# Overflow blocks moved behind the last expert's combine and written out, first rows turned ahead of two tables

## The reference, cut to what matters

```
g_sel = argmax(softmax(xf @ w_group + b_group))                 # 1 of 4 groups
top_w, top_i = top_k(softmax(e_logits of that group), 2)        # 2 of its 4 experts
for e in range(16):
    h = silu(xf @ w_gate[e]) * (xf @ w_up[e])                   # 2048 -> 512
    y = y + combine[:, e:e + 1] * (h @ w_down[e])               # 512 -> 2048
```

## Time and profile before

| | us |
|---|---|
| median of 3 runs (lowest, highest) | 1303.7 (1301.46, 1304.48) |
| the profiled execution, its own time | 1306.76 |
| its span, first to last instruction | 1304.8 |
| PE busy | 1225.2 (94%) |
| DVE busy | 490.5 (38%) |
| ACT busy | 190.3 (15%) |
| POOL busy | 51.1 (4%) |
| DMA, mean over the span | 254 GB/s |

### The profile page before, as it was taken

The page is one execution under the profiler, slowest core; times in us unless marked ns, Lnnn a source line. Parts: engine busy times, 40 slices in busy tenths (PEclk is TensorE's granted clock), DMA queues, the critical chain, the costliest instruction groups (busy, mean ns, idle before and its releaser), DMA issues.

```text
span 1304.8 us, 13620 instructions
## 1 busy us (share of the span) xinstructions
PE 1225.2 (94%) x5624; PEld 587.2 (45%) x5624; DVE 490.5 (38%) x958; ACT 190.3 (15%) x397; POOL 51.1 (4%) x67
## 2 busy tenths in 40 slices
PE   6999999999999977999997979999999999999995
PEld 4344443344444454777785764333333333333331
DVE  4000175199555543022215551333333333333334
ACT  2012223300222342000023330000000000000000
POOL 0002000000000012100000001000000000000000
PEclk8999999999989979999998977999999999999997
DMA  7835423445323258643365349999999999999941
GB/s 242 322 129 139 137 98 103 155 162 163 127 97 111 97 200 343 256 141 129 129 195 224 134 164 361 427 428 428 426 427 426 427 426 428 425 426 428 428 194 74
DMA packets 71130, 332.01 MB, mean 254 GB/s; under 512 B 13564, under 2 KB 17436, under 8 KB 54492
## 3 DMA queue, kind: packets, MB, share of 16 engines
q1 hardware_dynamic: 54624, 282.65, 55.2%
q0 software_dynamic: 8464, 41.42, 8.4%
q10 hardware_dynamic: 7980, 7.05, 2.2%
HBM read 320.61 MB, written 10.49 MB: 254 GB/s over the span
## 4 chain that ended last, share of the span: by engine, by line
PE 78%; DMA 9%; DVE 8%; ACT 3%; issue 2%; POOL 0%; DVEq 0%; ACTq 0%
PE PS L651 19%; PE PS L1210 15%; PE PS L944 14%; DMA ring<-in_w_up 7%; PE PS L1267 7%; PE PS L1174 4%; PE PS L628 3%; DVE X L1813 2%; DVE top L1812 2%; PE PS L769 1%; PE PS L892 1%; PE PS L1256 1%; PE PS L1178 1%; DMA X<-in_cache_v,ids 1%; PE PS L647 1%
## 5 line engine op out<-in xcount | busy, mean ns | idle before, releaser
L651 PE MATMUL PS<-ring,NC 128*128 128x512 f32 x704 | 323.7, 605 | 1.6 <-issue 1.6
L651 PEld LDWEIGHTS PS<-ring,NC 128*128 128x128 f32 x704 | 129.8, 192 | 155.0 <-issue 153.9
L944 PE MATMUL PS<-NC,ring 128*128 128x288 f32 x768 | 190.5, 407 | 1.6 <-issue 0.5
L1210 PE MATMUL PS<-ring,NC 128*64 128x512 f32 x768 | 178.9, 604 | 6.3 <-DMA ring<-in_w_up 4.8
L944 PEld LDWEIGHTS PS<-NC,ring 128*128 128x128 f32 x768 | 144.3, 190 | 42.0 <-issue 2.9
L2144 DVE TENSOR_TENSOR X<-X,PS 128x1024 f32<-128x1024 f32 x64 | 78.2, 1221 | 152.7 <-PE PS L1174 152.7
L1210 PEld LDWEIGHTS PS<-ring,NC 128*64 128x64 f32 x768 | 51.5, 138 | 126.9 <-issue 125.0
L1267 PE MATMUL PS<-ring,NC 128*64 128x512 f32 x384 | 85.0, 595 | 0.5 <-ACT NC L1699 0.5
L1697 ACT ACTIVATE NC<-PS,small 64x512 f32<-64x512 f32 x16 | 10.9, 680 | 439.7 <-PE PS L1210 439.7
L1174 PE MATMUL PS<-XNN,NC 64*128 64x512 f32 x256 | 72.3, 641 | 0.3 <-DVE XNN L2174 0.3
L1210 PE MATMUL PS<-XNN,NC 128*64 128x512 f32 x128 | 59.1, 599 | 2.6 <-DMA NC<-in_w_up 2.6
(11 more groups left out here) (404 smaller groups left out, 1089.6 us busy)
## 6 DMA issues: line engine op xcount, KB each, us to landing
ring<-in_w_gate SPq DMA_DIRECT2D x24, 2048.0 KB, 23.1
ring<-in_w_up SPq DMA_DIRECT2D x24, 2048.0 KB, 26.3
ring<-in_w_down SPq DMA_DIRECT2D x24, 2048.0 KB, 25.1
ring<-in_w_in SPq DMA_DIRECT2D x36, 1024.0 KB, 5.1
ring<-in_w_out SPq DMA_DIRECT2D x16, 1024.0 KB, 5.1
XNN<-in_w_gate SPq DMA_DIRECT2D x8, 2048.0 KB, 23.0
NC<-in_w_up SPq DMA_DIRECT2D x8, 2048.0 KB, 27.4
XNN<-in_w_down SPq DMA_DIRECT2D x4, 2048.0 KB, 23.7
```

Of the source, the lines that this page charges most:

```text
L651: last = mm(acc(n, t)[:, 0:width], lhs[:, kt, t * 128:(t + 1) * 128], slot(m)[:, k, 0:width], start=kt == 0, stop=kt == KT - 1)
L944: last = mm(PS[:, j, 0:NT], slot(m)[:, k, 128 * j:128 * j + 128], src[:, kt, :], start=kt == 0, stop=kt == width * 4 - 1)
L1210: last = mm(PS[64 * half:64 * half + 64, 2, :], XT[:, 4 * (kt // 4 % 2) + kt % 4, kt // 8, :], w, start=kt == 0, stop=kt == KT - 1)
```

## The change

1. On PE `rows_t(0)` stands ahead of the second slot table and the L1157 products, and DVE's first `lay_rows` ahead of its copy of that table. ACT waits for `route_ready` before its first SiLU.
2. On SP the wait for the stored rows moves from lot 4 to lot 6, that for the first gather from lot 6 to lot 7; the wait for the turned rows goes.
3. `star_down`, its copy and the combine and adds of the prompt's two halves come ahead of the overflow blocks; the samples' combine and adds stay behind them. A one-column memset on DVE behind the blocks counts up `y_ready`, and all six stores and the samples' combine wait for it.
4. The loops of PE, ACT, DVE and SP are eight tests and eight bodies written out, with constants in place of the loop's register.

```diff
@@ SP
-                    if lot == 4:
+                    if lot == 6:
                         sp.wait_ge(S("n_out"), 48)
-                    if lot == 6:
-                        sp.wait_ge(S("row_turned"), 12)
+                    if lot == 7:
                         sp.wait_ge(S("xg_in0"), 16)
...
-            with sp.Fori(0, NOVF) as b:
-                with sp.If(b < nov):
+            for b in range(NOVF):
+                with sp.If(nov > b):
...
-                sp.wait_ge(S("y_ready"), n + 2)
+                sp.wait_ge(S("y_ready"), max(n + 3, 6))
@@ PE
             slot_table(7, 0, NBLK).then_inc(S("tab_sum"), 1)
-            pe.wait_ge(S("hot_ready"), 3)
-            slot_table(4, NBLK, 3 * NBLK)
-            for c in range(4):
-                for n in range(6):
...
-            last.then_inc(S("tab_sum"), 1)
...
             rows_t(0).then_inc(S("xt_ready"), 1)
+            pe.wait_ge(S("hot_ready"), 3)
+            slot_table(4, NBLK, 3 * NBLK)
+            for c in range(4):
+                for n in range(6):
...
+            last.then_inc(S("tab_sum"), 1)
...
             combine_step(NEXP - 1, 4)
+            pe.wait_ge(S("ht_laid"), NEXP + 1)
+            star_down().then_inc(S("y_last"), 1)
+            pe.wait_ge(S("y_ready"), 1)
+            for t in range(2):
+                star_combine(t)
             pe.wait_ge(S("route_ready"), 1)
             nov = pe.value_load(ids_nov, min_val=0, max_val=NOVF)
-            with pe.Fori(0, NOVF) as b:
-                with pe.If(b < nov):
+            for b in range(NOVF):
+                with pe.If(nov > b):
...
+                    pe.wait_ge(S("y_ready"), 5)
...
-            pe.wait_ge(S("ht_laid"), NEXP + 1)
-            star_down().then_inc(S("y_last"), 1)
-            pe.wait_ge(S("y_ready"), 1)
-            for t in range(3):
-                if t == 2:
-                    pe.wait_ge(S("y_ready"), 3)
-                star_combine(t)
+            pe.wait_ge(S("y_ready"), 6)
+            star_combine(2)
@@ ACT
+            act.wait_ge(S("route_ready"), 1)
             for e in range(NEXP):
...
-            with act.Fori(0, NOVF) as b:
-                with act.If(b < nov):
+            for b in range(NOVF):
+                with act.If(nov > b):
@@ DVE
+            dve.wait_ge(S("xt_ready"), 1)
+            lay_rows().then_inc(S("xt_laid"), 1)
             dve.wait_ge(S("tab_sum"), 2)
...
+            dve.wait_ge(S("y_last"), 1)
+            V.tensor_copy(ysb[:, 0, 0:512], PS[:, 4, :]).then_inc(S("y_ready"), 1)
+            for t in range(2):
+                last_rows(t)
             nov = dve.value_load(ids_nov, min_val=0, max_val=NOVF)
-            with dve.Fori(0, NOVF) as b:
-                with dve.If(b < nov):
+            for b in range(NOVF):
+                with dve.If(nov > b):
...
+            V.memset(small[:, 200:201], 0.0).then_inc(S("y_ready"), 1)
+            last_rows(2)
```

More of the change, by code:

```diff
@@ L513, in _ @@
             sp.wait_ge(S("moe_free"), NLOT + NRING + 1)
-            with sp.Fori(0, NOVF) as b:
-                with sp.If(b < nov):
-                    e = sp.value_load(ids[0:1, bass.ds(b + 91, 1)], min_val=0, max_val=NEXP - 1)
+            for b in range(NOVF):
+                with sp.If(nov > b):
+                    e = sp.value_load(ids[0:1, 91 + b:92 + b], min_val=0, max_val=NEXP - 1)
                     for i, (wv, part) in enumerate(LOTS):
@@ L1151, in _ @@
             slot_table(7, 0, NBLK).then_inc(S("tab_sum"), 1)
-            pe.wait_ge(S("hot_ready"), 3)
-            slot_table(4, NBLK, 3 * NBLK)
-            for c in range(4):
-                for n in range(6):
-                    rows = ROWS[n % 3]
-                    last = mm(PS[32 * c:32 * c + 32, 4, 2 * NBLK:2 * NBLK + 3], row_hot[0:rows, n, 0:STAR],
-                              blk_tab[0:rows, n, NEXP:3 * NBLK:NBLK], start=n == 0, stop=n == 5)
-            last.then_inc(S("tab_sum"), 1)
             def rows_t(k):
@@ L1275, in _ @@
             rows_t(0).then_inc(S("xt_ready"), 1)
+            pe.wait_ge(S("hot_ready"), 3)
+            slot_table(4, NBLK, 3 * NBLK)
+            for c in range(4):
+                for n in range(6):
+                    rows = ROWS[n % 3]
+                    last = mm(PS[32 * c:32 * c + 32, 4, 2 * NBLK:2 * NBLK + 3], row_hot[0:rows, n, 0:STAR],
+                              blk_tab[0:rows, n, NEXP:3 * NBLK:NBLK], start=n == 0, stop=n == 5)
+            last.then_inc(S("tab_sum"), 1)
             for e in range(NEXP):
@@ L1703, in _ @@
             A(hTs, PS[:, 3, 0:4 * STAR].rearrange("p (f r) -> p f r", f=4), ACT.Copy).then_inc(S("ht_laid"), 1)
-            act.wait_ge(S("route_ready"), 1)
             nov = act.value_load(ids_nov, min_val=0, max_val=NOVF)
-            with act.Fori(0, NOVF) as b:
-                with act.If(b < nov):
+            for b in range(NOVF):
+                with act.If(nov > b):
                     act.wait_ge(S("moe_free"), b * NL + (NLOT + NRING + 1 + 4))
@@ L2121, in _, with lay_rows @@
             V.tensor_copy(tabF[:, 0:NBLK], PS[:, 7, 0:NBLK]).then_inc(S("tab_ready"), 1)
+            def lay_rows():
+                return TT(XT, PSF[:, 0:1024].rearrange("p (i h r) -> p i h r", i=8, h=2), gain_x, ALU.mult)
+            dve.wait_ge(S("gcol_in"), 16)
+            dve.wait_ge(S("xt_ready"), 1)
+            lay_rows().then_inc(S("xt_laid"), 1)
             dve.wait_ge(S("tab_sum"), 2)
@@ L2154, in combined @@
                     add_rows(s).then_inc(S("comb_free"), 1)
[L2157 to L2161, removed]
             for e in range(NEXP):
@@ L2180, in _, with last_rows @@
             combined(NEXP - 1, (4,))
+            def last_rows(t):
+                for x in range(2):
+                    dve.wait_ge(S("last_comb"), 2 * t + x + 1)
+                    at = (4, 0, 4)[t] + 2 * x
+                    out = hx[0:ROWS[t], t, 1024 * x:1024 * x + 1024].rearrange("p (h c) -> p h c", h=2)
+                    TT(out, out, PS[0:ROWS[t], at:at + 2, :], ALU.add).then_inc(S("y_ready"), 1)
+            dve.wait_ge(S("y_last"), 1)
+            V.tensor_copy(ysb[:, 0, 0:512], PS[:, 4, :]).then_inc(S("y_ready"), 1)
+            for t in range(2):
+                last_rows(t)
             nov = dve.value_load(ids_nov, min_val=0, max_val=NOVF)
-            with dve.Fori(0, NOVF) as b:
-                with dve.If(b < nov):
+            for b in range(NOVF):
+                with dve.If(nov > b):
                     dve.wait_ge(S("xt_ready"), b + (NEXP + 2))
                     lay_rows().then_inc(S("xt_laid"), 1)
-                    slot_weights(1, tabF[:, bass.ds(b + (NEXP + 1), 1)], tabF[:, bass.ds(b + (NBLK + NEXP + 1), 1)])
-                    TS(over_rs, cc("ones")[:, 0:1], tabF[:, bass.ds(b + (2 * NBLK + NEXP + 1), 1)], None, ALU.mult).then_inc(S("ov_rs"), 1)
+                    slot_weights(1, tabF[:, b + (NEXP + 1):b + (NEXP + 1) + 1], tabF[:, b + (NBLK + NEXP + 1):b + (NBLK + NEXP + 1) + 1])
+                    TS(over_rs, cc("ones")[:, 0:1], tabF[:, b + (2 * NBLK + NEXP + 1):b + (2 * NBLK + NEXP + 1) + 1], None, ALU.mult).then_inc(S("ov_rs"), 1)
                     dve.wait_ge(S("ov_silu"), b + 1)
```

## The result

The changed kernel takes 1328.4 us in the median of 4 runs (1326.5 to 1331.3), the kernel before 1302.7 us (1301.5 to 1304.5): ratio 1.0187, 95% interval 1.0155 to 1.022, 25.7 us between the medians. The forecast had the sign and both causes, but 1316.0 us and a range that ended at 1325.

What follows compares the result with a forecast made beforehand. The stream of weights was taken to limit the expert stage, whose start sets it one for one. Head +6.0 and tail +6.3 gave +12.3 us, a span of 1317.1, put onto the median as 1316.0 us; range 1304 to 1325.

Steps and rivals of the forecast that it cites:

- eight copies in place of a loop, on PE: Overflow blocks on PE: eight jumps over written-out bodies take 15.6 us, the chain ends at 1305.1, +6.3 us.
- a hop: PE's jump into a new instruction packet: 0.7 us until it is asked for plus 1.27 us transfer, 2.0 us.
- upper bound of 2.8 us: Most a jump on PE was given, from 16 KB issue to landing in the nearest row; 21 us in all.
- 7.6 hops: Number of jumps on PE charged 2.0 us each, the first packet being there; with 0.4 us, 15.6 us.
- Star_down: Products moved ahead of the overflow blocks: start at 1282.05, half run slow, 5.3 us, end at 1287.35.
- lower bound of 3.5: Least time for star_down, four column groups at L1267's pace: 3.5 us, against the 6.18 seen before.
- Tail: End of the kernel, from the moved overflow blocks and PE's eight jumps to the end of the span: +6.3 us.
- First rows turned first: Start of the expert stage: the tables now run behind the turned rows, so the gate product starts 6.0 us later.
- Lots asked for earlier: Weight loads ahead of the expert stage: net worth nothing, the gather gaining at most about 1 us.
- The stage goes one for one with its start: Expert stage: lot 8 goes by PE's first gate product, so its start sets the whole stage, one for one.
- the rivals with a free head: The later gate product costs nothing: with cheap jumps -3.8 us, 1299.9, chance 0.06; with dear jumps +6.3, 1310.0, chance 0.06.
- Cheap jumps: Rival: empty bodies on PE cost 0.4 us each and hide; tail -3.8, head +6.0, +2.2 us, 1305.9; chance 0.15.

Runs made afterwards that it cites:

- e7: The kernel before with PE's overflow loop alone written out eight times at its old place; ratio 1.013, +16.9 us.
- e11: The kernel before with only one test, nov > 0, around the overflow loop on each of four engines; ratio 0.995, 6.5 us faster.
- e2: The changed kernel with the edits around the first rows (points 1 and 2) undone; ratio 1.0135 to the kernel before, +17.6 us.
- e5: The changed kernel with PE's overflow bodies cut to about half, about 150 instructions; one execution, all eight tests take 15.2 us.
- e10: The kernel before with only the order of PE, VectorE and ScalarE changed around the first rows, SyncE's waits as before; ratio 1.0044, +5.7 us.
- e9: The kernel before with only SyncE's waits for the lots moved as in the change; ratio 1.003, +3.9 us.
- e4: The changed kernel with one test more, nov > 0, around PE's eight tests; ratio 1.0026 to the kernel before, +3.4 us.
- e6: The changed kernel with PE's overflow bodies cut to about 65 instructions; one execution, all eight tests take 4.2 us.

## Why the prediction was wrong in size and right in cause

*The step that failed: eight copies in place of a loop, on PE.* The count of the bodies in packets was near (some eight more were forecast), for the queue brought 53 packets where it had brought 46:

```profile
q8 instruction: 53, 0.87, 0.3%
```

The price of a hop was mis-sized: 0.7 + 1.27 = 2.0 us forecast, 3.41 us measured on the mean of eight, and the chain was 27.3 us long, not 15.6. Where the missing part lies can be read for the second jump, which starts at 1294.29. Instruction queue of the stretch 1294.2 to 1297.3, slices of 0.0775 us:

```profile
GB/s 0 0 0 0 106 0 0 0 0 0 211 0 0 0 0 0 0 0 0 0 0 0 0 0 0 0 0 0 317 370 370 476 370 423 423 370 370 423 264 529
...
q8 instruction: 1, 0.02, 1.9%
```

The packet starts in the eleventh slice, 1294.98, 0.7 us after the start of the jump (my 0.7 us had been read from the end of one), and takes 1.9% of 16 engines in 3.1 us, 0.94 us. The jump is over at 1297.29, 1.4 us after the packet. That last part, the 1.4 us between the packet and the end of the jump, had no row before, because no jump of before had to wait for its packet. I took the transfer for the whole wait; the upper bound of 2.8 us, from a transfer of the same size on another queue, was below it as well. Besides, the first packet was not there (3.57 us against 0.4), and all eight jumps were dear, where the sum had 7.6 hops, a number that the forecast doesn't derive. At the old place the first packet was there (0.37 us in e7 and e11), and with half bodies at the new place too, so it depends on how the body lies in the packets.

*Star_down* ran at full speed (granted clock 1.00), 3.6 us and not 5.3, near the forecast's lower bound of 3.5. That is the luck of this execution: at the same place it took 4.4 to 5.1 us in e2 to e5, at a granted clock of 0.71 to 0.82. With it, PE's tests began 2.1 us sooner than reckoned. Tail in all: +6.3 forecast, +16.5 measured; 11.7 from the jumps, -2.1 from the earlier start, and 0.6 from the last adds and stores at 6.6 us.

*First rows turned first:* +6.0 forecast; the order alone gave +5.7 in e10. Right.

*Lots asked for earlier:* worth nothing, or 1 us of gain for the gather, was the forecast. They cost 1.5 us in the profile of the changed kernel, set against the gather's 6.1 us of before (it landed after 5.1 to 6.9 in the kernels with the old waits), and e9 is slower by more than the uncertainty. The forecast had seen that the stores of the rows share the bus and put it at nothing, since the gather waits for the first table anyway; it overlooked that lot 6 waits for them. The last store took 10.2 us in place of 3.7, so lot 6 went out at 775.84, which is 781.4 in the time of before, and not at 774.6. It then filled the DMA engines in front of the gather: the bus was not free by 782, it was just then carrying lot 6.

*The stage goes one for one with its start:* right. From the first gate product to the last expert's it took 443.2 to 445.6 us in all thirteen kernels, wherever it began, so the rivals with a free head fall. The stream of weights is the limit only late in the stage, though: all six of PE's waits for weights in the kernel before lie behind 1050 us, one an expert and 1.1 to 1.4 us each. Until then the lots loaded ahead cover the stream's 30.7 us an expert, and PE's own 29.2 set the pace.

*Cheap jumps:* fell as a forecast, but priced the tail well. With the head, and with one dear jump that is over before VectorE's adds are, e4 is 3.4 us slower than before (interval 0 to 6.8); the rival said 2.2. The Trainium skill's compare-and-branch of some 108 ns (Advanced Engine Details and Errata, Control Flow Timing) is not what PE shows: 0.21 to 0.22 us where the code is at hand (0.37 for the first of a row), 2.1 to 4.9 us where it isn't. What the Trainium skill (Runtime: NRT & Kernel Launch, Instruction fetch mechanics) says of taken branches out of the window is borne out by e4, e5 and e6, but it gives no price.

## What to carry to other kernels

Written-out conditional code isn't free when it is skipped: what counts is how many skipped bodies leave the 16 KB of instructions at hand, here 3.4 us each on PE. Put one test around the whole, and keep the loop if its body stays resident. When a wait for data is being used to do other work, turning the order round pays the other work in full; look first at what runs inside the wait.

When the needed part of a price has no row before the change, such as a wait that never happened, the bound from similar transfers can lie below it; the range must then reach well over it.

## What the runs showed of the hardware

A jump over eight bodies, 8.8 packets by the count of the prediction, costs 3.66 us; one over a single body costs 2.9 to 3.8 us in the changed kernel and e2. Of seven or eight dear jumps in a row one takes 4.5 to 4.9 us, with stores beside it (the third in the changed kernel and in e2) and without (e7's seventh); half bodies had it at the sixth jump, 4.7 us, so it isn't a jump that passes a whole packet. In the changed kernel and with half bodies the extra time lies ahead of the packet, which starts 2.2 and 2.4 us after the jump, where the changed kernel's other seven start after 0.5 to 1.0. What sets it is open. On VectorE the same eight tests took 56 to 72 ns each in the changed kernel; its bodies are of eleven instructions besides their waits, and no run varied their size:

```profile
L2193 DVEq COMPARE_BRANCH  x8: 56/56/72, 1292.7 to 1294.5; - x8
```

The gather landed 5.1 to 8.5 us after its issue. Where lot 6 was ahead of it, it landed the later the closer lot 6 was; where it wasn't, the spread was still 5.1 to 6.9, and what sets that is open. Where the 2 us of e9 beyond its profile come from stays open too.
